# Moving small work between engines in a two-block forward pass: softmax scaling to GpSimd, context squares to ScalarE, modulation blocks to another phase

## Time and profile before

| what | value |
|---|---|
| median of 3 runs | 2138.36 us (2131.72 to 2143.5) |
| the profiled execution | 2134.92 us, span 2133.1 us |
| TensorE busy | 1965.8 us (92%) |
| VectorE, ScalarE, GpSimd busy | 47%, 35%, 51% |
| mean granted TensorE clock | 0.956 of full speed |
| read from HBM | 265.86 MB, 127 GB/s over the span |

### The profile page before, as it was taken

One profiled execution on the slowest core, in us unless ns is written; L12 is line 12 of the kernel. 1 busy time (PEld: TensorE's weight loads), 2 busy tenths in 40 slices (PEclk: granted clock), 3 DMA queues, 4 the chain that ended last, 5 costly groups with the idle time before them and its releaser, 6 DMA issues.

```text
span 2133.1 us, 32899 instructions
## 1 busy us (share of the span) xinstructions
PE 1965.8 (92%) x13805; PEld 1732.1 (81%) x13805; DVE 1003.0 (47%) x1706; ACT 747.8 (35%) x1212; POOL 1077.8 (51%) x565
## 2 busy tenths in 40 slices
PE   3988899987999999989998999999899998879997
PEld 3756899986798778968776888888798997879997
DVE  7853454125483577484246111112547767473114
ACT  2214354323322552272232222222245525334442
POOL 7004588746344544304433444444367742776885
PEclk9779999988999999999998999999999999989998
DMA  6355577777412213102332223322345331554652
GB/s 148 100 153 178 203 248 254 253 271 232 160 60 84 66 31 121 58 31 89 115 103 79 93 71 96 117 84 75 99 149 159 110 100 39 173 165 143 181 168 82
DMA packets 285734, 274.01 MB, mean 128 GB/s; under 512 B 6458, under 2 KB 283460, under 8 KB 285332
## 3 DMA queue, kind: packets, MB, share of 16 engines
q1 hardware_dynamic: 282164, 265.94, 39.1%
q10 hardware_dynamic: 2688, 4.86, 0.8%
q0 software_dynamic: 736, 1.12, 0.4%
HBM read 265.86 MB, written 4.19 MB: 127 GB/s over the span
## 4 chain that ended last, share of the span: by engine, by line
PE 82%; DVE 9%; ACT 2%; DMA 2%; issue 2%; POOL 1%; SPq 0%; DVEq 0%; ACTq 0%; POOLq 0%
PE gb L2332 18%; PE gb L2333 17%; PE gb L2334 17%; PE gb L1351 4%; PE gb L1353 3%; PE gb L1352 3%; PE gb L1559 3%; PE gb L1560 3%; PE gb L1558 3%; PE mb L2469 1%; PE mb L612 1%; PE mb L1099 1%; DVE mx L1128 1%; DMA raw<-in_w_ada 1%; PE mb L1154 1%
## 5 line engine op out<-in xcount | busy, mean ns | idle before, releaser
L2320 POOL TENSOR_TENSOR wl<-raw,wh 128x1024 fp32r<-128x1024 f32 (+3 forms) x452 | 982.4, 2192 | 927.2 <-ACT wh L731 926.4
L731 ACT CAST wh<-raw 128x1024 fp32r<-128x1024 f32 (+3 forms) x452 | 418.6, 937 | 756.6 <-PE gb L2334 384.8
L2332 PE MATMUL gb<-xh,wh 128*128 128x256 f32 (+1 forms) x1856 | 609.0, 328 | 20.1 <-DVE xl L1045 10.4
L2333 PE MATMUL gb<-xl,wh 128*128 128x256 f32 (+1 forms) x1856 | 605.5, 326 | 0.0
L2334 PE MATMUL gb<-xh,wl 128*128 128x256 f32 (+1 forms) x1856 | 604.9, 326 | 0.0
L2332 PEld LDWEIGHTS gb<-xh,wh 128*128 128x128 f32 x1856 | 358.1, 193 | 55.1 <-issue 19.0
L2333 PEld LDWEIGHTS gb<-xl,wh 128*128 128x128 f32 x1856 | 358.2, 193 | 27.6
L2334 PEld LDWEIGHTS gb<-xh,wl 128*128 128x128 f32 x1856 | 357.9, 193 | 27.9
L1351 PE MATMUL gb<-wh,xh 128*128 128x256 f32 x608 | 174.4, 287 | 1.4 <-POOL wl L2320 1.4
L1353 PE MATMUL gb<-wl,xh 128*128 128x256 f32 x608 | 172.8, 284 | 0.0
L1352 PE MATMUL gb<-wh,xl 128*128 128x256 f32 x608 | 172.7, 284 | 0.0
(11 more groups left out here) (447 smaller groups left out, 3050.6 us busy)
## 6 DMA issues: line engine op xcount, KB each, us to landing
raw<-in_w_in SPq DMA_DIRECT2D x62, 1024.0 KB, 5.3
raw<-in_w_ada SPq DMA_DIRECT2D x48, 1024.0 KB, 6.8
raw<-in_w_ffn SPq DMA_DIRECT2D x44, 1024.0 KB, 5.1
raw<-in_mlp_w SPq DMA_DIRECT2D x32, 1024.0 KB, 6.2
raw<-in_w_ffn SPq DMA_DIRECT2D x16, 768.0 KB, 4.6
raw<-in_w_ffn SPq DMA_DIRECT2D x16, 640.0 KB, 4.2
raw<-in_ssm_w_glu SPq DMA_DIRECT2D x8, 1024.0 KB, 6.9
raw<-in_w_out SPq DMA_DIRECT2D x8, 1024.0 KB, 5.1
```

The costliest lines, as they stand in the source:

```text
L731: nc.scalar.copy(split_half(wh, p, j, h), raw_half(p, it, j, h)).then_inc(hi_ready, 1)
L2320: nc.gpsimd.tensor_tensor(split_half(wl, p, j, h), raw_half(p, it, j, h), split_half(wh, p, j, h).bitcast(F32), ALU.subtract)\
L2332: nc.tensor.matmul(o, H[:, k, :], XH, start=st, stop=False)
L2333: nc.tensor.matmul(o, H[:, k, :], XL, start=False, stop=False)
```

## The change

- Four modulation blocks that stood behind ple's blocks 1, 3, 5, 7 are put behind mlp2's blocks 2, 6, 10, 14 (INLINE). The count between the phases stays; the blocks that follow move up in number.
- GpSimd squares only the first half of the context (two squares, one sum); ScalarE squares the other half into `sqr` and `cxsq2`, right after its second context copy, and in ple it no longer splits a conv block before that (`split_first=False`). TensorE adds the four new tiles of squares with ones, eight more matmuls.
- The norms 3, 4, 6, 7 and the head norm of differential attention use the chain with tiles in PSUM; in norm 2 and in the head norm the last result too is left in PSUM, and the diagonals of norm 2 are made by three 128x256 products instead of six 128x128.
- In differential attention GpSimd multiplies the second map's inverse sum by -lambda and the map by that; VectorE's step becomes: inverses of item i-1, maxima of item i, difference of item i-1.

```
-        INLINE = [(name, i) for name, n in (("mlp1", 16), ("mlp2", 16), ("ple", 8)) for i in range(1, n, 2)]
+        INLINE = [(name, i) for name, n in (("mlp1", 16), ("mlp2", 16)) for i in range(1, n, 2)]
+        INLINE += [("mlp2", i) for i in (2, 6, 10, 14)]
...
             pe.wait_ge(s_cq, 1)
+            pe.wait_ge(s_ca, 2)
             for t in range(2):
                 for i in range(2):
-                    ins = nc.tensor.matmul(mb[:, t, 2:3], cxsq[:, 2 + i, t * P:t * P + P], ones[:, 0:1],
-                                           start=(i == 0), stop=(i == 1))
+                    nc.tensor.matmul(mb[:, t, 2:3], cxsq[:, 2 + i, t * P:t * P + P], ones[:, 0:1],
+                                     start=(i == 0), stop=False)
+                for i in range(4):
+                    sq = (sqr[:, i, SEQ:SEQ + CTX] if i < 2 else cxsq2[:, i - 2, :])[:, t * P:t * P + P]
+                    ins = nc.tensor.matmul(mb[:, t, 2:3], sq, ones[:, 0:1], start=False, stop=(i == 3))
...
-            if n in (0, 1, 5, 8):
-                T1.add(nc.vector.tensor_scalar(rs[:, 0, 0:nt], total, 1.0 / count, eps, ALU.mult, ALU.add))
-                T1.wait()
-                rsqrt_beside(T1, rs[:, 0, 0:nt], rs[:, 1, 0:nt], *(gb[:, 1, 448 + 8 * i:448 + 8 * i + nt]
-                                                                   for i in range(2)), wide=dg[:, 0:nt, :])
-            else:
-                rsqrt(T1, rs[:, 0, 0:nt], rs[:, 1, 0:nt], rs[:, 2, 0:nt], rs[:, 3, 0:nt], total, 1.0 / count, eps,
-                      dg[:, 0:nt, :])
+            T1.add(nc.vector.tensor_scalar(rs[:, 0, 0:nt], total, 1.0 / count, eps, ALU.mult, ALU.add))
+            T1.wait()
+            ps = gb[:, 1, 448:464] if n in (0, 1, 5, 8) else mb[:, nt - 1, 448:464]
+            rsqrt_beside(T1, rs[:, 0, 0:nt], rs[:, 1, 0:nt], ps[:, 0:nt], ps[:, 8:8 + nt], wide=dg[:, 0:nt, :])
...
-            rsqrt_beside(T1, six[0], six[1], *(gb[:, 1, 448 + 8 * i:454 + 8 * i] for i in range(2)))
+            inverse = gb[:, 1, 464:470]
+            rsqrt_beside(T1, six[0], six[1], *(gb[:, 1, 448 + 8 * i:454 + 8 * i] for i in range(2)), last=inverse)
+            y = inverse.rearrange("p (t c) -> p t c", c=3)
+            wide = ident.unsqueeze(1).to_broadcast([P, 2, P])
             for c in (1, 2):
-                for t in range(2):
-                    T1.add(v.tensor_scalar(dg2[:, 2 * (c - 1) + t, :], ident, y[:, t, c:c + 1], None, ALU.mult))
+                T1.add(v.tensor_tensor(dg2[:, 2 * (c - 1):2 * c, :], wide, y[:, :, c:c + 1].to_broadcast([P, 2, P]),
+                                       ALU.mult))
...
+        def diff_pool(pool, l, P1):
+
+            for n in items(l, "d"):
+                c = ITEMS[n][5]
+                pool.wait_ge(s_r2, diff_index(n) + 1)
+                p1 = probs[:, (c + 1) % PROBS, 0:nk(n)]
+                P1.add(nc.gpsimd.tensor_tensor(mx[:, 2, (c + 1) % 8:(c + 1) % 8 + 1],
+                                               mx[:, 2, (c + 1) % 8:(c + 1) % 8 + 1], lamb[:, l:l + 1], ALU.mult))
+                P1.wait()
+                nc.gpsimd.tensor_tensor(p1, p1, mx[:, 2, (c + 1) % 8:(c + 1) % 8 + 1].to_broadcast([P, nk(n)]),
+                                        ALU.mult).then_inc(s_p1, 1)
...
-                D1.add(v.tensor_scalar(p1, p1, mx[:, 2, (c + 1) % 8:(c + 1) % 8 + 1], lamb[:, l:l + 1],
-                                       ALU.mult, ALU.mult))
-                D1.wait()
+                dve.wait_ge(s_p1, diff_index(n) + 1)
                 v.scalar_tensor_tensor(p0, p0, mx[:, 2, c % 8:c % 8 + 1], p1, ALU.mult, ALU.add).then_inc(s_wd, 1)
 
             for i in range(len(mine) + 1):
+                if i >= 1:
+                    difference(mine[i - 1])
                 if i < len(mine):
                     for c in scores_of(mine[i]):
                         row_maximum(dve, mine[i], c)
                 if i < 2:
                     transposes_dve(dve, l, "d", 4 + 2 * i, 6 + 2 * i)
                 if i >= 1:
-                    difference(mine[i - 1])
+                    weighted(mine[i - 1])
...
-                rsqrt(D1, st[:, 1, 0:n], st[:, 2, 0:n], st[:, 3, 0:n], st[:, 0, 0:n], st[:, 0, 0:n], 1.0 / P, EPS)
+                step(v.tensor_scalar(st[:, 1, 0:n], st[:, 0, 0:n], 1.0 / P, EPS, ALU.mult, ALU.add))
+                inverse = mb[:, 3, 384:512][:, 64:64 + n]
+                rsqrt_beside(D1, st[:, 1, 0:n], st[:, 2, 0:n], mb[:, 3, 384:512][:, 0:n], mb[:, 3, 384:512][:, 32:32 + n], last=inverse)
...
+                if 4 * it + j == 7:
+                    act.wait_ge(s_cxc, 2)
+                    for i, dst in enumerate((sqr[:, 0:2, SEQ:SEQ + CTX], cxsq2[:, :, :])):
+                        nc.scalar.activation(dst, x[:, 4 + 2 * i:6 + 2 * i, SEQ:SEQ + CTX], ACT.Square)\
+                            .then_inc(s_ca, 1)
             gemm_act(act, p_pl, pair_tanh(act, p_pl, SEQ), context_copy,
-                     lambda: squares_act(act, 2, sqr))
+                     lambda: squares_act(act, 2, sqr), split_first=False)
...
-                    for f in range(0, KD, 2):
+                    for f in range(0, KD // 2, 2):
                         if f == 0:
                             pool.wait_ge(s_cxt, 2)
-                        if f % 4 == 0:
-                            pool.wait_ge(s_cxc, f // 4 + 1)
+                            pool.wait_ge(s_cxc, 1)
```

More of the change, by code:

```diff
@@ L240, in build @@
         dg1 = at("dg1", [P, 2, P], F32, offset=cx_at + 4096)[0]
+        cxsq2 = at("cxsq2", [P, 2, CTX], F32, offset=cx_at + 5120)[0]
         PROBS = 6
@@ L403, in build @@
         s_rc = sem("sums_inverted")
+        s_r2 = sem("pair_of_sums_inverted")
+        s_p1 = sem("second_map_scaled")
         s_go = sem("pair_output_multiplied")
@@ L424, in build @@
         s_cq = sem("context_squares_ready")
+        s_ca = sem("context_squared_by_scalar")
         s_pl = sem("p_lo")
@@ L901, in rsqrt, with rsqrt_beside @@
                 step(v.scalar_tensor_tensor(y, t, 1.5, y, ALU.add, ALU.mult))
-        def rsqrt_beside(T1, ms, y, yp, t, wide=None):
+        def rsqrt_beside(T1, ms, y, yp, t, wide=None, last=None):
             def step(ins):
@@ L918, in rsqrt_beside @@
                     return
-                step(v.scalar_tensor_tensor(yp if i < 2 else y, t, 1.5, y, ALU.add, ALU.mult))
+                step(v.scalar_tensor_tensor(yp if i < 2 else y if last is None else last, t, 1.5, y,
+                                            ALU.add, ALU.mult))
         def rms_dve(dve, T1, n, dg, count, eps):
@@ L954, in first_rms_dve @@
             T1.wait()
-            rsqrt_beside(T1, six[0], six[1], *(gb[:, 1, 448 + 8 * i:454 + 8 * i] for i in range(2)))
+            inverse = gb[:, 1, 464:470]
+            rsqrt_beside(T1, six[0], six[1], *(gb[:, 1, 448 + 8 * i:454 + 8 * i] for i in range(2)), last=inverse)
+            y = inverse.rearrange("p (t c) -> p t c", c=3)
+            wide = ident.unsqueeze(1).to_broadcast([P, 2, P])
             for c in (1, 2):
-                for t in range(2):
-                    T1.add(v.tensor_scalar(dg2[:, 2 * (c - 1) + t, :], ident, y[:, t, c:c + 1], None, ALU.mult))
+                T1.add(v.tensor_tensor(dg2[:, 2 * (c - 1):2 * c, :], wide, y[:, :, c:c + 1].to_broadcast([P, 2, P]),
+                                       ALU.mult))
             T1.wait()
             dve.sem_inc(s_dg, 1)
-            for t in range(2):
-                T1.add(v.tensor_scalar(dg1[:, t, :], ident, y[:, t, 0:1], None, ALU.mult))
+            T1.add(v.tensor_tensor(dg1[:, 0:2, :], wide, y[:, :, 0:1].to_broadcast([P, 2, P]), ALU.mult))
             T1.wait()
@@ L1285, in difference, with weighted @@
                 dve.wait_ge(s_ex, c + 2)
-                D1.add(v.reciprocal(mx[:, 2, c % 8:c % 8 + 2], mx[:, 1, c % 8:c % 8 + 2]))
-                D1.wait()
+                if diff_index(n) >= 4:
+                    dve.wait_ge(s_p1, diff_index(n) - 3)
+                v.reciprocal(mx[:, 2, c % 8:c % 8 + 2], mx[:, 1, c % 8:c % 8 + 2]).then_inc(s_r2, 1)
+            def weighted(n):
+                c = ITEMS[n][5]
                 p0, p1 = probs[:, c % PROBS, 0:nk(n)], probs[:, (c + 1) % PROBS, 0:nk(n)]
-                D1.add(v.tensor_scalar(p1, p1, mx[:, 2, (c + 1) % 8:(c + 1) % 8 + 1], lamb[:, l:l + 1],
-                                       ALU.mult, ALU.mult))
-                D1.wait()
+                dve.wait_ge(s_p1, diff_index(n) + 1)
                 v.scalar_tensor_tensor(p0, p0, mx[:, 2, c % 8:c % 8 + 1], p1, ALU.mult, ALU.add).then_inc(s_wd, 1)
             for i in range(len(mine) + 1):
+                if i >= 1:
+                    difference(mine[i - 1])
                 if i < len(mine):
@@ L2317, in turn @@
                                     grouped_pool(pool, l)
+                                if p is L2[l]["b", 1]:
+                                    diff_pool(pool, l, P1)
                         for h in range(2):
```

2 lines of the change are left out of this document (1 added, 1 removed).

## The result

The changed kernel takes 2122.16 us in the median of 6 runs (2117.49 to 2124.22), beside 2135.49 of the kernel before (6 runs, 2131.72 to 2143.5): a ratio of 0.9929, 95% interval 0.991 to 0.9949. Run again later on another occasion it took 2117.44 (ratio 0.9909, 0.9887 to 0.9931). Faster, as forecast; the forecast was 2118.6. On the shown median of 2138.36 the two ratios make 2123.2 and 2118.9: the first is what rivals 2 and 4 gave (2123 and 2124), the second the forecast, so the time alone doesn't tell them apart. The profiled execution took 2121.33 us, span 2119.5: 13.6 less than the one before, where the sum of the prediction says 19.7.

A forecast was written before the change was run, and what follows sets the result against it. TensorE was taken as the bound (82% of the chain of waits), so gains come only where it stands still. 4.4 - 14.8 - 2.3 - 3.2 - 2.8 - 1.0 = -19.7 gave 2118.6 us, range 2109 to 2130.

The forecast's parts named there:

- Rival 2: First norm keeps a hidden end: transfers land 3 us late or the clock drops in ple; 2123 us, chance 0.20.
- rival 4: Less everywhere: GpSimd's phases shift and stalls return elsewhere around the norms; -14, 2124 us, chance 0.13.
- Modulation blocks in mlp2, +4.4: Second MLP product: four modulation blocks added there cost 4.4 us, with no TensorE stall for transfers.
- Rival 1: mlp2's transfers become the bound: four dense stretches each stop TensorE 2 us, ple gains only 12; 2129 us, chance 0.12.
- Ple and first norm, -14.8: Gated-embedding phase and layer 0's first norm: conv starts at 526.0 instead of 540.82, -14.8 us (-11 to -17).
- The sums: First norm on TensorE: 44 instructions at 0.11 after dense work, 4.9 us against 6.8 before.
- The step with two SBUF inputs: First norm's VectorE chain: one step may wait for a GpSimd subtraction, +0.5 us (0 to 2.5).
- FFN norms, -2.3 and -3.2: FFN norms of layers 0 and 1: PSUM chain takes 2.65 us instead of 4.94 and 5.84, with TensorE waiting for both.
- Head norm and layer 1's attention, -2.8 and a part of -1.0: Layer 1: head norm 9 us shorter, removing TensorE's 2.83 wait, -2.8; attention there shares the -1.0 for both layers.
- Differential attention, -1.0 in all: Attention stages: GpSimd scales the second map, TensorE then binds at period 2.45 instead of 2.64; -1.0 us (-3 to +3).
- path (a): Attention loop: VectorE's inverse, GpSimd's two products, then VectorE's difference, together 2.3 us, not binding.
- rival 3: Slower: GpSimd closes the attention loop, period 4.6 instead of 2.64 us; 2163 us, chance 0.05.

The follow-up runs named there:

- a_ada: Kernel before with only the four modulation blocks moved from ple to mlp2: 2138.81 us, ratio 1.0015 to the kernel before.
- h_no_ada: Changed kernel with the four modulation blocks put back behind ple's blocks: 2116.24 us, ratio 0.9887 to the kernel before.
- f_merge: Kernel before with only the head norm of differential attention on the PSUM chain: 2134.68 us, ratio 0.9971.
- b_ctx: Kernel before with only the context part (ScalarE squares half, no early conv split, 8 more TensorE products): 2131.19 us, ratio 0.9977.
- d_diff: Kernel before with only differential attention changed (GpSimd scales the second map, VectorE's new order): 2127.17 us, ratio 0.9967.
- r_after: The changed kernel itself, unchanged, run again on another occasion: 2117.44 us, ratio 0.9909 to the kernel before.
- k_early2: h_no_ada with the modulation blocks inside norms 0 and 1 moved behind mlp1's blocks 4 and 8: 2112.15 us, ratio 0.9875 to the kernel before.
- m_early2_adds: k_early2 with VectorE adding the context squares as well: 2116.13 us, ratio 0.9902 to the kernel before.
- c_norms: Kernel before with only the norm chains changed (tiles in PSUM, diagonals as 128x256, head norm included): 2122.11 us, ratio 0.9944.
- g_dve_adds: Changed kernel with VectorE adding the eight context squares down to two tiles: 2114.39 us, ratio 0.9893 to the kernel before.
- n_early3_adds: m_early2_adds with the last modulation block also taken out of its norm, behind mlp1's block 12: 2113.52 us, ratio 0.9887 to the kernel before.

## Why the prediction was right, and where not

The time lay in the range because most of the mechanisms were right and the misses partly cancelled: ple and conv's start brought 5.8 us less than forecast and layer 0's FFN norm 1.6 less, the stretch of layer 1's attention and head norm more. That some of the latter was a matter of which execution was profiled, as the table shows, is luck. The first conv matmul came 2.6 us earlier in the span, 5.8 without the start, and not about 10.5.

Rival 2 came true in part: the clock fell, though among the sums and not in ple, and the last modulation block was no hidden end (it ran at 526.76 right behind the sums). Of rival 4 one stall came back, 2.16 us in layer 0's first norm, and none in the FFN norms.

- **Modulation blocks in mlp2, +4.4.** Right in size: the four cost 4.7 (8.0 late at 465.26, 3.3 at the phase's start), with no wait of TensorE. Rival 1 is out. The rate was reckoned wrong: at the prediction's own prices four weight blocks and three modulation blocks take 4 x 5.8 + 3 x 1.1 = 26.5 us, not 27.6, which makes 277 GB/s and not 266; the trace has 26.6 (398.1 to 424.7), and still no wait. A pair of them:

```profile
405.08 1.07 PE L617 MATMUL mb<-raw,sc 128*32 128x256 f32 x16
412.02 1.07 PE L617 MATMUL mb<-raw,sc 128*32 128x256 f32 x16
```

- **Ple and first norm, -14.8: the term that was too large.** The sums began where forecast: 519.48 is 511.1 once the 8.4 us are taken off by which this execution was late at 483. From 483 to 538 the stretch lost 11.0 us, and conv's start gave 2.0 back. Three terms were mis-sized. The sums: 7.2 for 4.9, since "TensorE comes from dense work, so I take half, 0.11" held only to 522, where the clock fell to the lower of its levels among one-column products. The step with two SBUF inputs: 2.16 for 0.5, within the bounds given. And the lower clock in conv's first 4 us, +2, stands in no term. 2.3 for the sums, 1.5 for the chain (5.4 with the step in it, where 3.9 was forecast) and 2.0 are the 5.8 that are missing. The diagonals (0.75, forecast 0.84), the context copy's wait (1.10) and the vanished 4.58 us wait were right.
- **Which part earns it.** The prediction let ple's gain hang on the moved blocks. a_ada and h_no_ada show the opposite: the context part alone (ScalarE's order and GpSimd's smaller share) brings conv from 540.82 to 531.50, and the move costs a few us net, alone as well as beside the others. Every term of mine for the move had compared it with the kernel before, none with the other edits already made; two edits that free the same wait earn it once.
- **FFN norms, -2.3 and -3.2.** In layer 1 3.3 (3.2 to 3.3 in every profile with the new chain). In layer 0 the chain itself did as forecast, 2.63 instead of 4.94, but TensorE gained 0.7. VectorE's first and last step, and the sums ahead of them:

```profile
1151.02 0.17 DVE L918 TENSOR_SCALAR mb<-rs 128x4 int32<-128x4 int32 x1
...
1153.65 0.69 DVE L926 SCALAR_TENSOR_TENSOR dg<-mb,rs 128x512 f32<-128x512 f32 x1
```
```profile
1147.12 3.57 PE L875 MATMUL mb<-ones,sqr 128*128 128x1 f32 x16 [1.31 <-ACT sqr L813]
```

  The sums took 1.95 in the one execution before. Where they take 3.57, the old chain starts later against GpSimd's two subtractions and stalls once, not twice: in f_merge, which has the old chain, L892 took 1.72 us and L893 did not stall, and a_ada, b_ctx and d_diff are alike. The value of removing a stall depends on where the other engine is, and I had one execution.
- **Head norm and layer 1's attention, -2.8 and a part of -1.0:** 7.8 in this profile. The head norm's term was right: 3.0, the wait of 2.83 and what belongs to it. The attention ahead of it has -0.8, and 3.1 of the remaining 4 us are the two stretches at the lower clock that the one execution before had and this one hadn't; a_ada and b_ctx, without either edit, differ by 3.1 from 1772 to 1911.
- **Differential attention, -1.0 in all: the second term that was mis-sized.** 7 us measured alone (3 to 11), 4.4 of them placed in the traces. The period is 2.39, forecast 2.45; but what closes it is not TensorE, it is path (a), from GpSimd's two products to VectorE's difference and the next inverse:

```profile
1788.02 0.19 POOL L1156 TENSOR_TENSOR mx<-mx,lamb 128x1 f32<-128x1 f32 x1 [1.08 <-DVE mx L1308]
1788.29 1.04 POOL L1159 TENSOR_TENSOR probs<-probs,mx 128x512 f32<-128x512 f32 x1
```
```profile
1787.77 0.17 DVE L1308 RECIPROCAL mx<-mx 128x2 f32<-128x2 f32 x1
...
1789.37 0.75 DVE L1314 SCALAR_TENSOR_TENSOR probs<-probs,mx 128x512 f32<-128x512 f32 x1
```

  GpSimd's prices were right (0.2 and 1.04 taken, 0.19 and 1.04 measured), so rival 3 is out. What I missed is the count: the items of the fill gain too (2.64 to some 2.3 each), the short items' period falls from 1.71 to 1.59 where I had 0, and the third period of layer 0, with the projections' transposes in it, gets shorter: 3.54 in the execution I read and 4.11 to 4.58 in the four others without this part, 2.29 in this profile and five others with it, but 3.39 to 3.73 in r_after, k_early2 and m_early2_adds.

The Trainium skill (SBUF — State Buffer, Who interferes with whom) has VectorE instructions with two SBUF inputs contend with a GpSimd instruction that reads SBUF, and those with at most one, outside the two-port modes, not. The 2.16 us step (two), the diagonals of c_norms inside GpSimd's window (one, 0.75) and the head norm's products (2.87 with two, 0.69 with one) agree; for two inputs in the new diagonals no run here shows it.

## What to carry to other kernels

Value each edit beside the others already made, not beside the old kernel: run the parts alone and leave each out once. Where one engine's small steps stall beside another's long instructions, the gain from ending the stall is set by their relative timing, so read it in several executions. And before a whole difference of two profiles is explained, subtract the stretch ahead of the first edit, and look at the same stretch in a kernel that has no edit there.

## What the runs showed of the hardware

A stalled VectorE instruction does its work when the GpSimd instruction under way has ended. Before, GpSimd's two subtractions ran to 1153.47 and VectorE's step L893 to 1153.50; in r_after the four ran to 527.65 and the step L959 to 527.67. Larger instructions end later by more of their own work: the diagonals of the earlier trace rows stall twice, to 533.03 and 535.33 beside subtractions that end at 532.95 and 535.25, and the head norm's product of 128x512 ends 0.55 us behind its subtraction (1824.39 and 1823.84). A step that happens to begin just before a subtraction ends pays nothing: in the kernel before the step with two SBUF inputs took 0.17 us at 528.23, with subtractions ending at 528.35.

```profile
1151.24 2.26 DVE L893 TENSOR_SCALAR rs<-rs 128x4 int32<-128x4 int32 x1
```
```profile
1148.83 4.64 POOL L2320 TENSOR_TENSOR wl<-raw,wh 128x1024 fp32r<-128x1024 f32 x2 [11.41 <-ACT wh L731]
```
```profile
525.32 2.35 DVE L959 SCALAR_TENSOR_TENSOR rs<-rs 128x2 f32<-128x2 f32 x1
```
```profile
518.36 9.29 POOL L2352 TENSOR_TENSOR wl<-raw,wh 128x1024 fp32r<-128x1024 f32 x4 [3.74 <-ACT wh L736]
```

So a step of 0.17 us can cost up to one whole subtraction (9.29 for four), and the next one another. L893 has a single SBUF input: it is not only two-input instructions that stall.

TensorE's granted clock fell to its lower level among one-column products though TensorE was busy without a gap (519.48 to 526.7). In all 14 profiles it falls in these sums or within some 2.5 us ahead of or behind them and is back some time later, and conv's first matmuls are slow where they come before it is back:

| profile | wait ahead of the sums | clock at 0.50 | first conv matmul | 538 to 585 |
|---|---|---|---|---|
| before | 4.58 | 518.5 to 538.9 | 540.82, full clock | |
| d_diff | 5.06 | 517.2 to 537.6 | 539.32, full clock | 0.0 |
| c_norms | 5.20 | 522.4 to 542.9 | 539.31, half | +1.7 |
| after | none | 521.9 to 542.4 | 538.18, half | +2.0 |
| g_dve_adds | none | 519.9 to 530.1, 533.5 to 536.9 | 532.26, full clock | +1.6 |
| n_early3_adds | none | 512.5 to 522.7 | 524.31, full clock | 0.0 |

So it is not the wait ahead of the sums that decides: c_norms waits as long as d_diff. A norm that gets shorter can bring the next dense phase forward into the stretch at the lower clock and lose up to 2.7 us of the gain (1.4 to 2.7 in ten profiles). What ends that stretch was not settled.
